# The second block of a two-block model as one pipeline of 512-column chunks, with attention steps placed between input chunks

## The reference, cut to what matters

```python
def second_block(x, meta_tokens, norm_gain, w_in, w_branch_sb, w_branch_swa, w_out, attn_sinks, final_norm_gain):
    h = concatenate([pad, meta_tokens, x])                 # 112 of padding, 16 meta, 256 tokens
    xn = rms_norm_2(h, norm_gain)
    proj = xn @ w_in                                       # 1024 x 6400
    sb_q, sb_k, sb_v, sw_q, sw_k, sw_v, sb_z, sw_z, g_sb, g_sw = split(proj)
    # widths      512, 512, 512, 1024, 128, 128, 512, 1024, 1024, 1024
    o_sb = stick_breaking_attention(sb_q, sb_k, sb_v, valid)     # 8 heads of 64
    o_sw = sliding_window_sink_attention(rope(sw_q), rope(sw_k), sw_v, attn_sinks, valid)  # 16 heads, window 128
    y_sb = (o_sb * silu(sb_z)) @ w_branch_sb
    y_sw = (o_sw * silu(sw_z)) @ w_branch_swa
    merged = sigmoid(g_sb) * y_sb + sigmoid(g_sw) * y_sw
    return rms_norm_2(h + merged @ w_out, final_norm_gain)       # the 256 tokens
```

## Time and profile before

| what | value |
| --- | --- |
| three runs | 1684.99, 1681.27, 1683.6 us, median 1683.6 |
| profiled execution | 1687.16 us, its span 1685.3 us |
| busy in the span | PE 1579.1, DVE 1110.3, ACT 912.0, POOL 103.5 us |
| mean granted clock of TensorE | 0.949 of full speed |
| experts' last product; first product of the second block; last product | 1257.03; 1291.46; 1676 us |
| PE from first to last product of the second block | 364.77 of 385.00 us busy, clock 0.88 |

### The profile page before, as it was taken

One profiled execution on the slowest core, in us unless ns is written; L12 is line 12 of the kernel. 1 busy time (PEld: TensorE's weight loads), 2 busy tenths in 40 slices (PEclk: granted clock), 3 DMA queues, 4 the chain that ended last, 5 costly groups with the idle time before them and its releaser, 6 DMA issues.

```text
span 1685.3 us, 20057 instructions
## 1 busy us (share of the span) xinstructions
PE 1579.1 (94%) x8026; PEld 1355.0 (80%) x8026; DVE 1110.3 (66%) x918; ACT 912.0 (54%) x777; POOL 103.5 (6%) x117
## 2 busy tenths in 40 slices
PE   4989999988989999999999999999986999899897
PEld 3768998867788888888888888888865997577886
DVE  3886445359768888888888888897866350223444
ACT  4534443234437677767767677767753245534432
POOL 1800000035010000000000000001002000000000
PEclk9989999989989999999999999999996999668899
DMA  7436984343239999999999999999974341101240
GB/s 274 147 103 221 321 282 162 126 160 126 103 109 416 349 394 357 378 374 363 391 350 402 358 383 364 367 385 364 404 281 158 126 134 54 63 1 63 97 153 25
DMA packets 121904, 408.23 MB, mean 242 GB/s; under 512 B 5728, under 2 KB 42768, under 8 KB 121840
## 3 DMA queue, kind: packets, MB, share of 16 engines
q1 hardware_dynamic: 117600, 392.91, 63.7%
q0 software_dynamic: 3088, 10.22, 1.8%
q10 hardware_dynamic: 1152, 4.19, 0.6%
HBM read 399.96 MB, written 19.40 MB: 249 GB/s over the span
## 4 chain that ended last, share of the span: by engine, by line
PE 82%; DVE 9%; ACT 4%; DMA 2%; issue 2%; SPq 0%; POOL 0%; ACTq 0%; DVEq 0%; POOLq 0%
PE ps L461 24%; PE ps L463 24%; PE ps L462 24%; DVE yT L1645 4%; PE ps L457 2%; DVE low L445 1%; PE ps L2122 1%; ACT prob L717 1%; DMA raw<-in_w_in 1%; DVE xT_lo L1590 1%; DMA raw<-in_moe_wu 1%; PE ps L1083 1%; DMA ys<-eo 1%; PE ps L1117 0%; PE ps L1872 0%
## 5 line engine op out<-in xcount | busy, mean ns | idle before, releaser
L451 DVE TENSOR_TENSOR low<-raw,high 128x2816 fp32r<-128x2816 f32 (+1 forms) x168 | 516.4, 3089 | 100.4 <-ACT high L440 100.3
L440 ACT ACTIVATE high<-raw 128x2816 fp32r<-128x2816 f32 (+1 forms) x168 | 428.7, 2561 | 107.2 <-PE ps L463 49.6
L461 PE MATMUL ps<-high,xT_hi 128*128 128x512 f32 (+2 forms) x1216 | 456.3, 375 | 31.7 <-DVE xT_lo L1590 17.2
L463 PE MATMUL ps<-high,xT_lo 128*128 128x512 f32 (+2 forms) x1216 | 449.9, 370 | 0.0
L462 PE MATMUL ps<-low,xT_hi 128*128 128x512 f32 (+2 forms) x1216 | 448.6, 369 | 0.0
L461 PEld LDWEIGHTS ps<-high,xT_hi 128*128 128x128 f32 x1216 | 231.3, 190 | 67.5 <-DVE xT_lo L1590 19.0
L445 DVE TENSOR_TENSOR low<-raw,high 128x2816 fp32r<-128x2816 f32 (+2 forms) x72 | 202.9, 2825 | 98.5 <-ACT high L434 98.2
L463 PEld LDWEIGHTS ps<-high,xT_lo 128*128 128x128 f32 x1216 | 231.2, 190 | 32.4
L462 PEld LDWEIGHTS ps<-low,xT_hi 128*128 128x128 f32 x1216 | 231.7, 191 | 31.3
L434 ACT ACTIVATE high<-raw 128x2816 fp32r<-128x2816 f32 (+2 forms) x72 | 168.7, 2346 | 147.9 <-PE ps L463 134.3
L461 PE MATMUL ps<-high,eT_hi 128*128 128x512 f32 x352 | 142.1, 404 | 0.0
(11 more groups left out here) (342 smaller groups left out, 1675.6 us busy)
## 6 DMA issues: line engine op xcount, KB each, us to landing
raw<-in_moe_wg SPq DMA_DIRECT2D x64, 1408.0 KB, 8.2
raw<-in_moe_wu SPq DMA_DIRECT2D x64, 1408.0 KB, 9.3
raw<-in_moe_wd SPq DMA_DIRECT2D x48, 1536.0 KB, 8.6
rawb<-in_w_in SPq DMA_DIRECT2D x20, 1280.0 KB, 6.0
raw<-in_w_in SPq DMA_DIRECT2D x16, 1024.0 KB, 5.5
raw<-in_moe_wd SPq DMA_DIRECT2D x16, 1024.0 KB, 8.3
raw<-in_ffn_wg SPq DMA_DIRECT2D x8, 1408.0 KB, 9.8
raw<-in_ffn_wu SPq DMA_DIRECT2D x8, 1408.0 KB, 10.7
```

The costliest lines, as they stand in the source:

```text
L440: nc.scalar.activation(high[:, j % SPLITS, 0:n], raw[:, j % RAWS, 0:n], ACT.Copy).then_inc(hi_made, 1)
L451: nc.vector.tensor_tensor(low[:, j % SPLITS, 0:n], raw[:, j % RAWS, 0:n], f(high[:, j % SPLITS, 0:n]), ALU.subtract).then_inc(lo_made, 1)
L461: nc.tensor.matmul(out, xh, wh, start=first, stop=False)
L463: return nc.tensor.matmul(out, xl, wh, start=False, stop=last)
```

## The change

- **Chunks.** `w_in` is cut in 25 chunks of up to 512 columns: 4 row tiles x 512, so two chunks for 512 columns; one chunk (6) has all 8 row tiles x 256 columns, for the keys and values of the sliding window. Chunks 0, 1: stick-breaking values; 2, 3: keys; 4, 5: queries; 6: keys and values; 7 to 14: sliding-window queries and gates; 15 to 24: gates.
- **Meta tokens.** Their norm and transposes move from the second block's start into the first block: ACT and DVE norm them before the first chunk's splits, PE transposes them in the first mixer behind chunk j = 2, and ACT and DVE split them there. They lie as columns 256 to 271 of `xTm_hi`/`xTm_lo`, of which `xT_hi`/`xT_lo` are now the first 256. No third tile is left: 16 meta columns ride as part of the moving operand (`columns`, 272 wide) or as a 16-column stationary operand (`meta_values`).
- **Keys and queries** of stick-breaking attention are made transposed (`columns`: the weight is the stationary operand), without PE transposes after.
- **Order.** One hand-written order on PE has an attention step between each two chunks (`fill`). Sliding-window attention goes in 8 half steps of 4 heads, each with a chunk. Stick-breaking attention's intermediates are written in place, in two buffers.
- **ACT tables.** One set that holds Exp and Ln is loaded once, for the whole of the attention; gates are copied as they are, and Silu comes in one go behind the last exponentials, then Sigmoid.
- **Start and end.** The first two weight chunks are loaded and the first three split before the experts' last result is back (`add_moe` stands behind them). The output stage works off pairs of chunks, one token half after the other. `keep_warm` remains with 16 and 20 transposes.

The diff, cut to its core:

```diff
-SLOTB = 2560
-BCH_IN, BCH_SB, BCH_SW, BCH_OUT = 20, 2, 4, 4
-Q2W = 320
+SLOTB = 2048
+BCH_IN, BCH_SB, BCH_SW, BCH_OUT = 25, 2, 4, 4
...
+    xTm_hi = place("xTm_hi", [P, KT, TM], F32R)
+    xTm_lo = place("xTm_lo", [P, KT, TM], F32R)
+    xT_hi, xT_lo = xTm_hi[:, :, 0:T], xTm_lo[:, :, 0:T]
...
     def second_loads(sp, n_items):
...
-        sp.wait_ge(lo_made, chunk(n_items, 0))
-        for c in range(BCH_IN + BCH_SB + BCH_SW + BCH_OUT):
-            if c >= RAWSB:
+        for c in range(CHUNKS2):
+            if c < 2:
+                sp.wait_ge(lo_made, chunk(n_items, 0) - 3 + c)
+            elif c >= RAWSB:
                 sp.wait_ge(blo_made, c - RAWSB + 1)
...
             def mixer(l):
                 c0 = LAYER_CHUNKS * l
                 high_upto(c0 + 3)
+                if l == 0:
+                    act.wait_ge(mt_filled, 1)
+                    nc.scalar.activation(xTm_hi[:, :, T:TM], ps[:, 6, T:T + KT * META].rearrange("p (t n) -> p t n", t=KT),
+                                         ACT.Copy).then_inc(mt_hi_made, 1)
...
                         mm.then_inc(prep_filled, 1)
+                        if l == 0:
+                            pe.wait_ge(meta_made, 1)
+                            for k in range(KT):
+                                mm = nc.tensor.transpose(ps[:, 6, T + k * META:T + k * META + META], xm[:, k * P:k * P + P],
+                                                         ident[0:META, 0:META])
+                            mm.then_inc(mt_filled, 1)
...
+        def columns(c, banks, width):
+            pe.wait_ge(blo_made, c + 1)
+            wh, wl = wide(c)
+            for t in range(4):
...
+                for k in range(4):
+                    kt = 4 * (c % 2) + k
+                    o, cols = ps[:, banks[t], 0:width], slice(t * P, t * P + P)
+                    nc.tensor.matmul(o, wh[:, k, cols], xTm_hi[:, kt, 0:width], start=kt == 0, stop=False)
+                    nc.tensor.matmul(o, wh[:, k, cols], xTm_lo[:, kt, 0:width], start=False, stop=False)
+                    mm = nc.tensor.matmul(o, wl[:, k, cols], xTm_hi[:, kt, 0:width], start=False, stop=kt == KT - 1)
...
-        for w in range(4):
-            gate_block(w, 0)
-            pt_fill(w, 0)
-            pt_fill(w, 1)
-            sw_output(w, 0)
-            if w < 3:
-                sw_scores(w + 1)
-            pt_fill(w, 2)
-            sw_output(w, 1)
-            gate_block(w, 1)
-            pt_fill(w, 3)
-            sw_output(w, 2)
-            sw_output(w, 3)
...
+        for c in range(2):
+            mm = meta_values(c, 3, 0, 4, W2)
+        keep_warm(2, 16)
+        values()
+        pe.wait_ge(mv_read, 1)
+        columns(2, K_BANKS, TM)
+        columns(3, K_BANKS, TM)
+        columns(4, Q_BANKS, T)
+        columns(5, Q_BANKS, T)
+        sb_scores(0)
+        keys_values()
+        sb_scores(1)
+        fill(7)
+        sb_suffix(0)
+        fill(8)
+        sb_output(0)
+        sb_suffix(1)
+        sb_scores(2)
...
+        for h in range(8):
+            pt_fill(h, 0)
+            if h + 2 < 8:
+                sw_scores(h + 2)
+            pt_fill(h, 1)
+            if h == 7:
+                sw_transposes(0)
+            fill(16 + h)
+            sw_output(h)
+        sb_transposes()
+        fill(24)
+        sw_transposes(1)
...
+        keep_warm(SB_OUT[2], 20)
+        for pair in range(2):
+            c0 = CHUNKS2 - BCH_OUT + 2 * pair
+            for b in range(NB):
+                if pair == 0:
+                    merged_transposes(b)
...
+                for n in range(2):
...
+                    mm = branch_block(c, b, (t, t + 1), xT_hi, xT_lo, SW_OUT, pair == 0 and n == 0, pair == 1 and n == 1)
```

1255 lines of the change are left out of this document (698 added, 557 removed).

## The result

The changed kernel takes 1627.95 us (median of four runs, 1626.91 to 1636.89) against 1683.95 us before (four runs): the ratio is 0.9674, with a 95% interval from 0.9647 to 0.9701. The forecast was 1615 us with a range from 1597 to 1645. So it went the way of the forecast, 13 us short of it. The profiled execution took 1627.22 us, its span 1625.3 us, 10.0 us over the 1615.3 forecast for it; that is the number taken apart here.

What follows compares the result with a forecast made beforehand. PE was taken as the bound, busy 1579.1 of 1685.3 us. Second block -87.5, first mixer +6.5 and clock +11 gave -70: span 1615.3, execution 1617.2, median 1613.6, rounded up to 1615 us; range 1597 to 1645.

Steps and rivals of the forecast that it cites:

- The second block as a sum of products and attention steps: Second block added up anew from the costs of products and attention steps: -87.5 us against 1685.3.
- The cover: Attention: the 5.44 us chunk behind each step covers ACT and DVE; 0 for waits, other end +23.
- The first mixer: First block: sigmoid and chunk 4's low part wait for meta transposes, diagonals start near 51.5; +6.5 us, ends 0 and +10.
- The clock: Second block: light stretches between dense chunks bring the clock down, 4 to 5 drops; +11 us, ends 0 and +25.
- Rival A: Whole kernel: the clock never falls; 1604 us, with a free first mixer 1597; chance 0.14.
- Rival B: Attention: clock low through most of it, 90 us of light steps at half speed; 1657 us; chance 0.11.
- rival C: Second block: clock low from first interleaved step to end of half steps, chunks included; some 1786 us; chance 0.04.
- the row at 1418: Kernel before, 1418.2 to 1425.1: PE busy all 6.90 us at clock 0.51, back within one chunk.
- The values: Second block: 48 products, 10.9 us, and 2 for half clock at the start.
- The start: Second block: values start as soon as one token half is there, 5 us earlier, at 1286.5.
- their loads cost 0: Second block's start: early loads cost 0 while a quarter of the DMA's time is in use.
- Rival D: Interleaved stages: ACT or DVE becomes the bound; +23, 1638 us; chance 0.20 together with splits that do not gain.

Runs made afterwards that it cites:

- fourth run: Changed kernel with the outputs of each sliding-window half step put ahead of its chunk instead of behind it: 1657.94 us, ratio 0.9860.
- first run: Changed kernel with ACT's meta copy behind the first mixer's sigmoid and chunk 4's high part, DVE's cols copy ordered behind it: 1617.74 us, ratio 0.9614.
- the second: Changed kernel with DVE's cols, meta split and wsT ahead of chunk 4's low part in the first mixer, ACT's order left: 1629.32 us.
- ninth run: Changed kernel once more, unchanged, in one job with two later kernels: 1635.08 us, ratio 0.9705.
- sixth: Changed kernel with each gate tile activated as it is read from PSUM, the Exp and Ln table set loaded back behind it: 1637.11 us.
- twelfth: Kernel with the later meta copy and both attentions' outputs dealt out, plus chunk 2's load held until the experts' result is back, its split behind the transposes: 1602.43 us.
- fifth run: Changed kernel with each sliding-window half step's outputs dealt out among the products of its chunk's second half: 1627.79 us.

## Why the prediction was right, and where it was off

**What held.** The second block as a sum of products and attention steps at full clock is near what it takes when the clock stays up: 94.2 us forecast for the loop and 95.3 measured, 133.3 and 135.6 for the stage ahead. The cover held too: waits for ACT and DVE within the attention are 1.7 us, and the fourth run shows what they would have been. The differences of the table add up to the 10.0 us: 6.4 in the first block, 0.7 at the start, -1.7 in the values, 3.4 and 10.3 in the two stages of attention, 1.0 and 0.9 behind them, less the 11 of the clock. The transposed queries and keys, the meta tokens without a tile of their own and the values took what the products cost.

**The first mixer, +6.5 forecast and +12.9 measured,** is the step that was mis-sized, and 6.4 of the 10.0 us. The mechanism was as told: the wait for the meta transposes holds the sigmoid, it the high part, that the low part, `cols`, `wsT` and the diagonals. Two sizes were off. The diagonals started at 53.27, not 51.5, as the transposes ended near 45.2, not 44, and the table load and the split took their full time in a row. And I took their 28.7 us as given. They took 32.1. They now stood under DVE's splits and convolution from their first moment; of the kernel before and of the changed kernel:

```profile
45.80:60.00 14.20, 14.20 (x69) 11.81 (x68) 9.13 (x12) 5.85 (x5) 14.19 (x17) 1.00 0.60 208
```

```profile
53.30:67.40 14.10, 14.10 (x67) 11.57 (x66) 13.81 (x32) 7.18 (x9) 14.10 (x14) 1.00 0.74 272
```

POOL worked on 17 of them in 14.2 us before, while DVE was busy for 9.1, but on 14 in 14.1 us now, while DVE was busy for 13.8. The first run goes with this (17 in 14.1 us, DVE busy for 9.2), and the second (31.4 us for all 31, begun early but under more of DVE's work); that DVE is the cause is argued from these rows and not tested by itself. The 10 us end of the bound was too near for a chain of four late steps.

**The clock, +11 forecast.** Against the same stretches at 1.00 in other kernels the profiled run lost 9.2 us in the loop (104.5 against 95.3) and 1.1 ahead of it (136.7 against 135.6), 10.3 in all. The number of drops, four, is as forecast, but the size is right by luck: the forecast had drops in all stretches alike, and the runs show them behind most runs of output matmuls on 16-row values in the loop (two to four of four in each profile) and a matter of chance in the stage ahead, where 0.9 to 10.3 us were lost over the runs. The ninth run, the same kernel, lost 9.2 us more there and has a median 20 us above the forecast; it is still inside the range. Rival A, a clock that never falls while PE is busy, is refuted by the windows around 1460 and by the ninth run. Rival B, low through most of the attention, and rival C didn't come; each time the half step's chunk brought the clock back before its end, as the row at 1418 had said. Rival B was also priced too low, at half of its 90 us: the transposes and scores of one half step took 3.3 us at full clock (from 1448.04 to 1451.30) and 5.9 at half (from 1459.84 to 1465.69), 0.8 of their length more.

The Trainium skill's page "TensorE: Matmul & The Clock Gate", section "HAM oscillation — how this bites in real kernels", names idle gaps between bursts as what lowers the clock. The windows of the changed kernel don't agree: it fell behind 8.00 of 8.00 us of busy time. Falls beside a gap, as the section has them, show in the loop of the fourth run, the sixth and the twelfth. The same Trainium skill page, section "Part 4: PE-mode transpose", says that transposes do not count as busy in the same way. The runs here speak against it: in the fifth run two sets of four transposes stand in each light stretch as before, and the clock stays at 1.00, and with 20 transposes ahead of the merge it was 1.00, where it was 0.70 with a wait of 1.5 us in their place.

**Smaller terms.** A chunk between attention steps takes 5.66 us from its first start to the next step's, not 5.44, as the change between the kinds costs some 0.2; over 17 chunks some 3.7 us, of which the forecast had none. The values took 11.2 us, not 12.9: of the 2 us for half clock at the start the profiled run had next to nothing. Behind PE 8.5 us remained, not 7.6: DVE did start its last adds 1.5 us closer to PE's end, but the last output DMA took a us longer. The start cost 0.7 more, behind which stand a result that comes back 7 us later and a larger gain from the early splits; the forecast's "their loads cost 0" was wrong: the quarter of the DMA's time in use was a mean over the block, and these loads stood beside the result's own way. The twelfth run gives 4.5 us of it back.

**Rival D,** ACT as the bound, is not seen in the changed kernel; it shows in the sixth run, where ACT has 14 us more to do (67.4 and 58.0 in place of 62.1 and 49.1), in the loop alone.

## What to carry to other kernels

A change that moves one small step into another stage has to be followed through the queue of every engine that takes part, with the engines at the end of the chain priced by what they will then run beside: 0.3 us of copying cost 9.5 us here (8 to 12 over all profiles). Short matmuls between dense ones are worth dealing out among them, one or two at a time, when their own run is some 3 us: the same work took 95.3 in place of 104.5 us, and with the outputs of both attentions dealt out the spread between runs fell from 10.0 to 3.3 us. And a median can hide a gain of 9 us behind chance in another stage, so compare the stretch that the edit touches.
